# A 32x32-tile inverse and a 24-tick slot for the RWKV recurrence of a two-block fp32 kernel

## The reference

```python
def step(s, inp):
    rt, wt, kt, vt, at, bt = inp
    sa = jnp.einsum('bhij,bhj->bhi', s, at)
    s = s * wt[:, :, None, :] + sa[..., None] * bt[:, :, None, :] + vt[..., None] * kt[:, :, None, :]
    y = jnp.einsum('bhij,bhj->bhi', s, rt) if with_out else None
    return s, y
# a = -kk, b = kk * sigmoid(a logits), kk = normalised k * k_k, w = decay, all per token and channel
```

## Time and profile before

| | us |
|---|---|
| median of 3 runs | 3738.09 |
| profiled execution, its time | 3748.26 |
| its span | 3746.4 |
| TensorE busy (share) | 3279.1 (88%) |
| VectorE busy | 1795.0 (48%) |
| ScalarE busy | 1098.1 (29%) |
| GpSimd busy | 161.1 (4%) |

### The profile page before, as it was taken

The page is one execution under the profiler, slowest core; times in us unless marked ns, Lnnn a source line. Parts: engine busy times, 40 slices in busy tenths (PEclk is TensorE's granted clock), DMA queues, the critical chain, the costliest instruction groups (busy, mean ns, idle before and its releaser), DMA issues. The chain is left out here.

```text
span 3746.4 us, 58412 instructions
## 1 busy us (share of the span) xinstructions
PE 3279.1 (88%) x26168; PEld 2484.4 (66%) x26168; DVE 1795.0 (48%) x2799; ACT 1098.1 (29%) x1660; POOL 161.1 (4%) x218
## 2 busy tenths in 40 slices
PE   4999987899979869888968989976889998798799
PEld 1443343598965358888866979763669797356598
DVE  1103356555562076676645555443645554454453
ACT  0012310133321043443311333336233332143232
POOL 2102011000000100000000000000000000200000
PEclk8998988899989979999978999986999999859899
DMA  8111444155533100000022545531425554304253
GB/s 241 67 46 68 151 142 157 68 182 179 197 109 119 39 2 3 3 3 3 3 75 81 195 149 187 181 124 40 140 90 180 166 183 147 112 1 136 89 180 135
DMA packets 249842, 409.56 MB, mean 109 GB/s; under 512 B 10055, under 2 KB 102616, under 8 KB 249464
## 3 DMA queue, kind: packets, MB, share of 16 engines
q1 hardware_dynamic: 244824, 390.49, 30.7%
q0 software_dynamic: 4768, 15.35, 1.7%
HBM read 400.77 MB, written 2.95 MB: 108 GB/s over the span
## 5 line engine op out<-in xcount | busy, mean ns | idle before, releaser
L341 DVE TENSOR_TENSOR ring_parts<-ring,arena_parts 128x2048 fp32r<-128x2048 f32 (+1 forms) x266 | 589.0, 2256 | 338.9 <-ACT arena_parts L334 336.6
L334 ACT CAST arena_parts<-ring 128x2048 fp32r<-128x2048 f32 (+1 forms) x266 | 487.2, 1882 | 582.9 <-PE psum L2072 229.5
L2072 PE MATMUL psum<-arena_parts 128*128 128x256 f32 x2816 | 511.8, 285 | 6.6 <-DVE arena_parts L450 6.3
L2072 PEld LDWEIGHTS psum<-arena_parts 128*128 128x128 f32 x2816 | 441.4, 193 | 9.3 <-DVE arena_parts L450 9.3
L493 PE MATMUL psum<-ring,hT 128*128 128x512 f32 (+1 forms) x960 | 417.3, 597 | 9.5 <-DVE hT L1242 2.6
L2072 PE MATMUL psum<-arena_parts,ring_parts 128*128 128x256 f32 x1408 | 399.5, 284 | 0.0
L378 PE MATMUL psum<-arena_parts 128*128 128x512 f32 x1184 | 367.1, 391 | 8.2 <-DVE arena_parts L2108 8.2
L493 PEld LDWEIGHTS psum<-ring,hT 128*128 128x128 f32 x960 | 185.3, 194 | 237.2 <-issue 224.2
L2072 PEld LDWEIGHTS psum<-arena_parts,ring_parts 128*128 128x128 f32 x1408 | 271.6, 193 | 0.0
L378 PEld LDWEIGHTS psum<-arena_parts 128*128 128x128 f32 x1184 | 223.0, 189 | 55.0 <-DVE arena_parts L2108 9.0
L1315 PE MATMUL psum<-arena_parts 128*128 128x512 f32 x768 | 240.5, 395 | 7.8 <-DVE arena_parts L1362 7.8
(11 more groups left out here) (485 smaller groups left out, 5154.4 us busy)
## 6 DMA issues: line engine op xcount, KB each, us to landing
ring<-in_mlp_w SPq DMA_DIRECT2D x48, 2048.0 KB, 7.9
ring<-in_ada_w SPq DMA_DIRECT2D x24, 2048.0 KB, 7.9
ring<-in_ffn_pre_w_gu SPq DMA_DIRECT2D x44, 1024.0 KB, 7.3
ring<-in_ffn_post_w_gu SPq DMA_DIRECT2D x44, 1024.0 KB, 7.7
ring<-in_ffn_pre_w_down SPq DMA_DIRECT2D x8, 2048.0 KB, 7.9
ring<-in_xmem_wkv SPq DMA_DIRECT2D x8, 2048.0 KB, 8.0
ring<-in_ffn_post_w_down SPq DMA_DIRECT2D x8, 2048.0 KB, 8.0
ring<-in_ab_w_in SPq DMA_DIRECT2D x7, 2048.0 KB, 7.8
```

Of the source, the lines that this page charges most:

```text
L334: nc.scalar.copy(high_view(name)[:, k, :], raw_view(name)[:, k, :]).then_inc(*up(act, ("high", name, h)))
L341: nc.vector.tensor_tensor(low_view(name)[:, k, :], raw_view(name)[:, k, :], high_view(name).bitcast(F32)[:, k, :], ALU.subtract)\
L2072: ins = nc.tensor.matmul(psum[:, b, 256 * j:256 * j + 256], s[:, k, at:at + P], x_parts[q][:, k, :], start=(k == 0 and i == 0), stop=(k == ...
```

## The change

Numbers of matmuls are those of the whole program.

1. **Near blocks and inverse.** Only the 32x32 diagonal blocks of each chunk matrix, and the block between them, are made for the inverse: `near_pe` multiplies B and A straight into four 32-partition quarters (1024 matmuls). The inverse runs on these in 14 steps, each for both directions, both heads and both blocks at once, 64 matmuls of 32x32 into one bank (7168 in place of 3584 of 64x64). The last two steps make the far block and add it into `TT`, into which GpSimd has put the diagonal blocks. Six of the 14 steps are copied by ScalarE (`COPIES_ACT`).
2. **Chunk products.** They hold 320 columns for a latent chunk and 192 for a context chunk, and only feed the walk. B and K transposed are products with the identity. One VectorE instruction masks each.
3. **Walk.** The state is no longer passed through TensorE by an identity product: GpSimd multiplies the old state with the chunk's decay, and VectorE adds the scaled new part. The first hop of a walk has no state.
4. **Order.** A slot has 24 ticks. `INV_STEPS` gives for each step its tick, left and right operand, destination and what is added. In tick t every engine does hop t of walk f-1, then the near blocks, inverse steps, chunk products of f and preparation of f+1 that the tables `INV_STEPS`, `GRAM_TICK` and `prep_*` put there. Products and inverse share four PSUM banks in turn, preparation has one. ScalarE's four Ln stand together, so that it changes its table less often.
5. **Buffers.** G of f even, B and K, and G of f odd lie in the three ring regions; R, A and the decays have three sets. The next slabs wait for walk 6 and the last chunk product of f=7, the third for walk 7.

The core of the diff:

```diff
+        TICKS = 24
+        WALK_ORDER = [(z, WALK[z][i]) for i in range(8) for z in range(2)]
+        GRAM_TICK = (3, 3, 5, 5, 7, 8, 8, 10, 10, 12, 12, 14, 14, 16, 16, 18)
+        INV_STEPS = (
+            (4, 1, 0, 2, None), (4, 0, 1, 3, None),
...
+            (17, FAR, 4, 3, None),
+            (19, 5, 3, "TT", "TT"),
+        )
+        COPIES_ACT = (1, 3, 4, 6, 8, 12)
-                for c in range(8):
-                    for h in HH:
-                        l = INV[f % 2][z][2 if left in ("off32", "off64") else left][h, c, :]
-                        rr = cst("eye64")[h, :] if right == "eye" else INV[f % 2][z][right][h, c, :]
-                        ins = nc.tensor.matmul(psum[h, b, 64 * c:64 * c + 64], l, rr, start=True, stop=True)
+                for n in range(16):
+                    for q in range(4):
+                        rr = cst("eye32")[Q4[q], :] if right == "eye32" else B[right][Q4[q], n, :]
+                        out_ = Q4[q ^ 1] if left == FAR else Q4[q]
+                        ins = nc.tensor.matmul(psum[out_, b, 32 * n:32 * n + 32], B[left][Q4[q], n, :], rr,
+                                               start=True, stop=True)
...
+                for c in range(8):
+                    for r, row in enumerate(HH):
+                        for half_ in range(2):
+                            s = Bh[f % 2][z][row, 64 * c:64 * c + 64].rearrange("p (a t) -> p a t", a=2)
+                            ins = nc.tensor.matmul(psum[Q4[2 * r + half_], b, 64 * c:64 * c + 64].rearrange("p (a t) -> p a t", a=2),
+                                                   A_[f % 3][z][row, c, 32 * half_:32 * half_ + 32],
+                                                   s[:, ::-1, :] if half_ else s, start=True, stop=True)
...
+                for r in HH:
+                    k_, b_ = Kh[f % 2][z][r, s], Bh[f % 2][z][r, s]
+                    if c < 4:
+                        nc.tensor.matmul(psum[r, b, 0:64], b_, R_[f % 3][z][r, c, :], start=True, stop=True)
+                        nc.tensor.matmul(psum[r, b, 64:192].rearrange("p (a t) -> p a t", a=2), k_,
+                                         RA[f % 3][z][r, :, c, :], start=True, stop=True)
+                    else:
+                        nc.tensor.matmul(psum[r, b, 128:192], k_, A_[f % 3][z][r, c, :], start=True, stop=True)
+                    nc.tensor.matmul(psum[r, b, 192:256], b_, cst("eye64")[r, :], start=True, stop=True)
+                    ins = nc.tensor.matmul(psum[r, b, 256:320], k_, cst("eye64")[r, :], start=True, stop=True)
...
-                if part == 2 and i < 7:
-                    act.wait_ge(*when(("S", "full", f, i, z)))
-                    c = WALK[z][i]
-                    nc.scalar.activation(St[z][(i + 1) % 2], walk_tile(z, 2), ACT.Copy,
-                                         scale=PC[f % 2][z][:, c:c + 1]).then_inc(*up(act, ("S", f, i + 1, z)))
+                    dve.wait_ge(*when(("S decayed", f, i, z)))
+                    ins = nc.vector.scalar_tensor_tensor(St[z][(i + 1) % 2], walk_tile(z, 2), PC[f % 3][z][:, c:c + 1],
+                                                         Sd[z], ALU.mult, ALU.add)
...
+        def slot_pe(pe, f):
+            for tick in range(TICKS):
+                walk_pe(pe, f - 1, tick)
+                near_pe(pe, f, tick)
+                inv_pe(pe, f, tick)
+                gram_pe(pe, f, tick)
+                prep_pe(pe, f + 1, tick)
...
+        def slot_dve(dve, f):
+            for tick in range(TICKS):
+                walk_dve(dve, f - 1, tick)
+                if tick in (15, 18, 21):
+                    walk_y(dve, f - 1, tick // 3 - 1)
+                near_dve(dve, f, tick)
+                inv_dve(dve, f, tick)
+                gram_dve(dve, f, tick)
+                prep_dve(dve, f + 1, tick)
+            walk_y(dve, f - 1, 7)
...
-                if 0 <= i - slab_at[("rw_o", 0, 0)] < RING:
+                if i in (FIRST_OUT, FIRST_OUT + 1):
                     sp.wait_ge(*when(("chains", 6)))
+                    sp.wait_ge(*when(("read", ("gram", 7, 1, 0))))
+                if i == FIRST_OUT + 2:
+                    sp.wait_ge(*when(("chains", 7)))
```

More of the change, by code:

```diff
@@ L1572, in prep_pe @@
             stage(pe, "prep")
-            if f == 0 and part == 0:
+            if f == 0 and tick == 0:
                 pe.wait_ge(*when(("dma", "w2")))
@@ L1592, in prep_pe @@
[L1592 to L1596, removed]
+            if tick < 4:
+                z, kind = divmod(tick, 2)
+                name, w, src = (("wl", w2_sb, t_w), ("al", a2_sb, t_a))[kind]
+                pe.wait_ge(*bank(4, (name, f, z)))
+                nc.tensor.matmul(psum[:, 4, :], w[HH[z], c], src[HH[z], :], start=True, stop=True)\
+                    .then_inc(*up(pe, (name, "full", f, z)))
@@ L1609, in prep_pe, with prep_act @@
                 ins.then_inc(*up(pe, ("coef", "full", f)))
-        def prep_act(act, f):
+        def prep_act(act, f, tick):
+            if f > 7:
+                return
             stage(act, "prep")
-            act.wait_ge(*when("rw columns"))
-            if f == 0:
+            if tick == 0 and f == 0:
+                act.wait_ge(*when("rw columns"))
                 act.wait_ge(*when(("dma", "VS")))
[L1616 to L1630, removed]
@@ new lines, in prep_act @@
+                act.wait_ge(*when(("used", FIRST_OUT - 1)))
+            if tick < 4:
+                z, kind = divmod(tick, 2)
+                name = ("wl", "al")[kind]
+                at = 16 * kind + 8 * z + f
+                act.wait_ge(*when((name, "full", f, z)))
+                nc.scalar.activation(tmp_[z][kind], psum[:, 4, :], ACT.Exp, bias=neg0[:, at:at + 1],
+                                     scale=-1.0).then_inc(*up(act, ("read", (name, f, z))))
+            if tick in (4, 5):
@@ L1642, in prep_act, with prep_dve @@
                 nc.scalar.activation(t[3], t[3], ACT.Exp, scale=KAPPA).then_inc(*up(act, ("decays", f, z)))
[L1643 to L1651, removed]
+        def prep_dve(dve, f, tick):
+            if f > 7:
@@ L1652, in prep_dve @@
                 return
             stage(dve, "prep")
[L1654 to L1655 removed]
+            if tick == 0:
                 if f == 0:
@@ new lines, in inv_pe @@
+        def inv_pe(pe, f, tick):
+            if f > 7:
+                return
+            stage(pe, "inv")
+            for i, (at, left, right, dst, add) in enumerate(INV_STEPS):
+                if at != tick:
+                    continue
+                b = AT[("inv", i)]
+                pe.wait_ge(*when(("inv start", f)))
+                for j in range(i):
+                    if INV_STEPS[j][3] in (left, right):
+                        pe.wait_ge(*when(("read", ("inv", f, j))))
+                pe.wait_ge(*bank(b, ("inv", f, i)))
+                for n in range(16):
[4 more added lines that the diff above has]
+                                               start=True, stop=True)
+                ins.then_inc(*up(pe, ("inv", "full", f, i)))
@@ new lines, in gram_dve @@
+        def gram_dve(dve, f, tick):
+            if f > 7:
+                return
+            stage(dve, "gram")
+            for i, (z, c) in enumerate(WALK_ORDER):
+                if GRAM_TICK[i] != tick:
+                    continue
+                b = AT[("gram", z, c)]
+                at = 0 if c < 4 else 128
+                dve.wait_ge(*when(("gram", "full", f, z, c)))
+                nc.vector.tensor_tensor(g_rows(f, z, c), psum[:, b, at:320], cst(f"gram{z}")[:, at:320], ALU.mult)\
+                    .then_inc(*up(dve, ("read", ("gram", f, z, c))))
@@ L2666, in _ @@
             proj_pe(pe)
[L2667 to L2673 removed]
+            for tick in range(TICKS):
+                prep_pe(pe, 0, tick)
+            for f in range(9):
+                slot_pe(pe, f)
             readout_pe(pe)
@@ L2878, in _ @@
             rw_pool(pool)
+            for f in range(9):
+                slot_pool(pool, f)
             readout_pool(pool)
```

510 lines of the change are left out of this document (259 added, 251 removed), and 7 rows, old and new, of the table INV_STEPS.

## The result

The changed kernel takes 3820.59 us (median of 4 runs, 3815.55 to 3822.8) against 3738.01 us for the kernel before in the same session: ratio 1.0216, 95% interval 1.0198 to 1.0234. It is 83 us slower; the prediction was 3620 us, and faster.

The account below looks back on a forecast made before the run. Bound: a chain that changes engine, walk in one half of a slot, VectorE's work in the other. Six slots save 87 us, first 13.6, last 17: 118 less, 3630, adjusted to 3620 for the runs' median; range 3570 to 3850.

Parts of the forecast that it names:

- Rates and Inverse: TensorE's inverse: 1792 records a slot at 8 ns, four row groups side by side, 14.3 us against 26.4 before.
- Each group's own work, not a common gate: TensorE's small matmuls: starts are spaced by each row group's own work; two groups can start within 0.01 us.
- New waits: All ticks of a slot: VectorE's excess adds 7.7 us and light ticks 1.5 to TensorE's 51.3, giving 60.5.
- Near blocks: New TensorE work before the inverse: 128 matmuls, 256 records a slot, 2 to 7.6 us, taken as 4.4.
- The other terms of TensorE's sum: TensorE per slot: near blocks 4.4, chunk products 10, walk 11.6, preparation 5.2, tile shape changes 5.8 us.
- VectorE, ScalarE, GpSimd: Work per slot: VectorE 37.4 us against 50.3, ScalarE 25 against 30.5; GpSimd's transfer 2.2 us, costing nothing.
- The slot without the supply limit: Full slot of the recurrent stage: 60.5 us predicted against 75 before, from 51.3 + 7.7 + 1.5.
- Slot 0: First slot of the recurrent stage, without walk: 46 us predicted against 59.6 before.
- slot 7: Last slot of the recurrent stage, without preparation: 48 us predicted against 65 before.
- Rival 1, the gate: Inverse's bursts: common gate on small matmuls, 24 ns a record, slot 86.8 us, 96 us more, 3834; chance 0.19.
- Rival 3, the clock: TensorE in the slots: clock at 1.2 GHz half the time, slot about 78, 18 us more, 3756; chance 0.09.
- Rival 2, hand-offs: Half a gain: 12 to 16 ns a record or uncovered matmul-copy hand-offs, slot about 70, 3699; chance 0.22.

Follow-up runs that it names:

- 64-column kernel: Changed kernel with each inverse matmul on 64 columns instead of 32, 32 matmuls a step instead of 64, inverse values not the reference's: 3601.45 us, 0.962 of the kernel before.
- 128-column matmuls: Changed kernel with each inverse matmul on 128 columns, 16 matmuls a step, inverse values not the reference's: 3597.48 us, 0.9613 of the kernel before.
- cols2: Changed kernel with its 64 inverse matmuls a step, each on 64 columns instead of 32, values not the reference's: 3794.82 us, 1.0147 of the kernel before.
- wide2inc: Changed kernel with 64-column inverse matmuls and four semaphore increments between them on TensorE's queue: 5650.73 us, 1.5101 of the kernel before.

## Why the prediction was wrong

The direction was wrong (0.72 on faster); the time lies in the range only because it reached to the gate's rival. Step by step:

- *Rates and Inverse.* Right in what was priced: 8 ns a record taken, 8.6 measured in a burst (9.7 over a slot's bursts). "Each group's own work, not a common gate" held inside the burst. But the sum multiplied that rate by 1792 records as if a burst could go on. 128 records take 1.1 us at this rate and arrive one block per 3.3 us or more: in the slot of 1500 to 1582 us the inverse kept TensorE for 19.8 + 15.9 = 36 us instead of 14.3, most of the extra as stops (columns as in the earlier trace rows; 1664 of the 1792 records are in this row):

```profile
L1819 PE MATMUL psum<-hT 32*32 32x32 f32 x1664 | 19.8, 204 | 15.9 <-issue 15.9
```

- **The step that failed** is the sum of *New waits*: "a tick costs the larger of TensorE's and VectorE's work, or one hop". A fourth limit was missing, the supply of TensorE's instructions. It stood in the profile of before: 29.5 ns a record is 3.8 us for 128, just above the 3.3 to 3.5 that the supply needs at the least, so the old inverse never showed it. The page's list of DMA queues had the instruction queue with 205 packets, and I never divided them by time. 1573 records a slot became 2690; the working has them part by part (1792, 256, 392 and the rest) and never as a sum to be delivered.
- *Near blocks.* The products with 64 columns took 1.93 us for 64 records in slot 0, where the clock is low, and 1.1 in the slots from 1664 us on, twice a slot; the 128 records of the third took 1.9 and 1.3 without a stop: 3.5 to 5.8 us against the 4.4 taken.
- *The other terms of TensorE's sum* (near blocks, chunk products, walk, preparation, tile shapes) add up to 37.0 us; in the 64-column kernel, at the upper clock, all but the bursts and stops took 38.
- *VectorE, ScalarE, GpSimd.* 37.4, 25 and 2.2 us predicted; 34.4, 23.0 and 1.9 (the transfer) measured, two table loads a slot, decayed states 0.44 us each. All hidden, as said.
- *The slot without the supply limit.* 60.5 us predicted, 55 measured with 64 columns: the uneven ticks (7.7 + 1.5 us) overlap better than taken. Slot 0 took 74 us (46 predicted), slot 7 67 (48), walk 7 alone 25 (27), preparation of f=0 31 (30): the two slots with less work beside the inverse lose 28 and 19 us, a full slot 22: their bursts were to follow each other faster, and could not.
- *Rival 1, the gate* (0.19): 3834 predicted at 24 ns, 3820.59 measured. Right size, wrong mechanism, so the agreement is luck: its limit "18.3 ns each" from which the change loses fits the average record (35.7 us for 1664, 21 ns), but what it would have shown, steps of 3 us evenly slow, isn't there, and 128-column matmuls gained nothing. The Trainium skill ("TensorE: Matmul & The Clock Gate", "Wait — 56ns, not 53.3ns?") says starts are never closer than about 25 ns; by the bursts (8.6 ns over 163 records in four row groups) the trace disagrees, and by the average over a slot's inverse, stops included, 21 ns, it does too.
- *Rival 3, the clock* (0.09): it did fall, to 0.74 to 0.86 in the slots, and by cols2 it costs at least some 26 us, a third of the 83. The stops alone don't bring it down: cols2 has as many and is granted 0.98 to 1.00 with twice the columns. *Rival 2, hand-offs*: refuted by the 64-column kernel; in the kernel before they are what is left once it is in fp16.

What stays open: how the supply works inside (why the next block is asked for only 1.2 us after the last one is begun), how much of the median distance of 3.74 us over the least of 3.29 is the supply's and how much work that happened to take longer, and how the 83 us divide between the supply and the lower clock.

## What to carry to other kernels

Before splitting matmuls into smaller tiles, count instructions, not only time: a record and its weight load are two, an fp32 matmul of this program four. The least distance between two blocks of 256 in any of these runs was 3.25 us, and where the supply was the limit the median was 3.7 to 3.8. By these figures, an estimate, a long stretch of N instructions takes N/256 x 3.3 to 3.8 us at the least, and the supply sets the time where the records are to start less than some 25 to 30 ns apart on average; put more columns into each matmul, use an operand type that needs one pass, or mix in work that is thin in instructions. In a trace it shows as stops "<-issue" in the middle of a group that waits for nothing, at multiples of 128 records, each shortly behind a packet of the instruction queue.

## What was not expected of the hardware

- Four row groups of 32x32 run at 8.6 ns a record, in fp32 and fp16 alike (128 fp16 records in 1.21 us), and a step was as fast in 16 matmuls of 128 columns as in 32 of 64.
- A semaphore increment on TensorE's queue costs 148 ns (wide2inc).
- Doubling the inverse's columns made the kernel 26 us faster, with a higher granted clock (0.93 for 0.77).
